# Three edits in TensorE's order of work: a product with its operands exchanged, a moved piece of a projection, two engines' copies exchanged

## What is computed

```
h = RMSNorm(x); proj = h @ w_in           # one projection for all groups
  retention:  rq, rk, rv, rg (4 heads)    # chunk 0: q, k; chunk 1: v, gate
  attention:  fq, fk, fv (8 heads)        # chunks 2, 3, 4
              fl = h @ w_in[:, 8 columns]
              logf = log_sigmoid(fl + fox_f_bias)
  conv:       cb, cc, ch
x = x + concat(retention, attention, conv) @ w_out
x = x + (silu(dwconv3(h2 @ w_gate)) * (h2 @ w_up)) @ w_down,  h2 = RMSNorm(x)
```

## Time and profile before

| | us |
|---|---|
| median of 3 runs | 1617.2 |
| lowest and highest | 1616.39, 1618.21 |
| the profiled execution's own time | 1618.32 |
| its span, first to last instruction | 1616.5 |
| PE busy | 1595.0 (99%), x10304 |
| PEld busy | 1389.9 (86%), x10304 |
| DVE busy | 1080.2 (67%) |
| ACT busy | 687.2 (43%) |
| mean granted TensorE clock | 0.999 |

### The profile page before, as it was taken

How to read it: one execution, slowest core, us unless ns; L and a number is a source line. 1 busy time by engine, 2 the same in 40 slices (tenths; PEclk the granted TensorE clock), 3 DMA queues, 4 the chain that set the end, 5 groups by cost and what they waited for, 6 DMA issues and landing times.

```text
span 1616.5 us, 29200 instructions
## 1 busy us (share of the span) xinstructions
PE 1595.0 (99%) x10304; PEld 1389.9 (86%) x10304; DVE 1080.2 (67%) x1749; ACT 687.2 (43%) x1285; POOL 410.8 (25%) x524
## 2 busy tenths in 40 slices
PE   7999999999999999999999999999999999999998
PEld 6878896688999999999888789867899999999997
DVE  4445447528977777777644553674399777777775
ACT  4224337416544444444433233463264444444442
POOL 1114200004433333333112140010044333333330
PEclk9999999999999999999999999999999999999999
DMA  8223423822222222222242224156213222222222
GB/s 247 79 50 87 137 85 105 301 78 66 79 78 78 85 83 81 90 89 78 72 110 66 70 80 144 66 178 227 85 60 105 85 87 88 78 78 78 78 78 71
DMA packets 125319, 160.04 MB, mean 99 GB/s; under 512 B 25636, under 2 KB 77294, under 8 KB 125166
## 3 DMA queue, kind: packets, MB, share of 16 engines
q1 hardware_dynamic: 125096, 158.65, 32.2%
q10 hardware_dynamic: 144, 0.33, 0.1%
HBM read 149.43 MB, written 9.53 MB: 98 GB/s over the span
## 4 chain that ended last, share of the span: by engine, by line
PE 94%; DVE 2%; ACT 1%; DVEq 1%; issue 1%; DMA 1%; POOL 0%; POOLq 0%; SPq 0%; ACTq 0%
PE bank L2156 89%; PE bank L2218 5%; DVEq L1837 1%; DVE pf L1840 1%; DMA raw<-in_w_in 0%; DVE xn L1505 0%; ACT pf L1284 0%; DMA raw<-in_w_gate 0%; DVE small L1827 0%; DVE hlo L1484 0%; DVE gulo L1484 0%; ACT xn L1152 0%; POOL small L923 0%; ACT hhi L1130 0%; POOLq L1046 0%
## 5 line engine op out<-in xcount | busy, mean ns | idle before, releaser
L2156 PE MATMUL bank<-whi,hhi 128*128 128x512 f32 x560 | 226.7, 405 | 2.4 <-ACT rso L1171 1.1
L2156 PE MATMUL bank<-whi,hlo 128*128 128x512 f32 x560 | 220.2, 393 | 0.0
L2156 PE MATMUL bank<-wlo,hhi 128*128 128x512 f32 x560 | 219.8, 393 | 0.0
L2156 PE MATMUL bank<-hhi,whi 128*128 128x320 f32 x640 | 199.2, 311 | 0.8 <-DVE hlo L1484 0.8
L2156 PE MATMUL bank<-hlo,whi 128*128 128x320 f32 x640 | 198.1, 310 | 0.0
L2156 PE MATMUL bank<-hhi,wlo 128*128 128x320 f32 x640 | 198.0, 309 | 0.0
L2156 PE MATMUL bank<-whi,guhi 128*128 128x512 f32 x440 | 174.1, 396 | 0.4 <-DVE gulo L1484 0.4
L2156 PE MATMUL bank<-wlo,guhi 128*128 128x512 f32 x440 | 173.8, 395 | 0.0
L2156 PE MATMUL bank<-whi,gulo 128*128 128x512 f32 x440 | 173.7, 395 | 0.0
L1460 DVE TENSOR_TENSOR wlo<-raw,whi 128x1024 fp32r<-128x1024 f32 x80 | 100.1, 1252 | 106.1 <-ACT whi L1079 104.8
L1943 DVE TENSOR_TENSOR x<-x,bank 128x512 f32<-128x512 f32 x220 | 143.1, 682 | 39.6 <-PE bank L2156 39.3
(11 more groups left out here) (312 smaller groups left out, 3662.1 us busy)
## 6 DMA issues: line engine op xcount, KB each, us to landing
raw<-in_w_in SPq DMA_DIRECT2D x52, 512.0 KB, 3.7
raw<-in_w_gate SPq DMA_DIRECT2D x44, 512.0 KB, 3.8
raw<-in_w_down SPq DMA_DIRECT2D x44, 512.0 KB, 3.7
vb<-in_cache_fox_v SPq DMA_DIRECT2D x16, 1024.0 KB, 6.8
raw<-in_w_up SPq DMA_DIRECT2D x24, 512.0 KB, 3.8
gains<-in_w_up SPq DMA_DIRECT2D x20, 512.0 KB, 3.8
raw<-in_w_out SPq DMA_DIRECT2D x16, 512.0 KB, 4.8
kb<-in_cache_fox_k SPq DMA_DIRECT2D x8, 1024.0 KB, 6.7
```

What stands on the lines that cost most here:

```text
L2156: return pe.matmul(out, lhsT=lhsT, rhs=rhs, start=start, stop=stop, skip_group_check=True)
```

## The change

Three edits.

**The product.** `fl` becomes one job in one bank. For each of the five token tiles, the tokens' 128 columns of `hhi` and `hlo` are stationary and the 16 columns of `wfl` stream: 80 matmuls with 16 columns in place of 32 with 320. The result is token-major at once; `flT`, its bank's job and the table `fsum` go. ScalarE copies the bank into `flr`, now 128 rows by 5 x 16, and VectorE adds the two parts and then the bias, from SBUF, with a drain between.

**The piece.** The piece of chunk 2 behind `retained(1)` goes, and one comes behind `fill(ins, "rso")`, ahead of `chunk2(0, [3])`. The iterator hands them out in the same order.

**The copies.** From step 2 of the cache sweep on, ScalarE copies the key groups 1 and 3 and VectorE 0 and 2; before, ScalarE 0 and 2 and VectorE 1 and 3.

```diff
@@ plan_banks @@
-    j(("fl", 0), 0)
-    j(("fl", 1), 2)
+    j("fl", 0)
     chunk(1)
     turns("rt")
-    j("flT", 7)
@@ the buffer of the copied product @@
-            [("flr", [2 * FH, NTOK], F32)],
+            [("flr", [P, TT, 2 * FH], F32)],
@@ ScalarE @@
-                for half in range(2):
-                    evac(("fl", half), flr[:, half * HALF:(half + 1) * HALF], l, view=lambda b: b[0:2 * FH, 0:HALF])
+                evac("fl", flr[:, :, :], l, view=lambda b: b[:, 0:TT * 2 * FH].rearrange("p (t n) -> p t n", t=TT))
...
-                        for p_ in (0, 2) if n > 1 else (2, 3) if n == 1 else ():
+                        for p_ in (1, 3) if n > 1 else (2, 3) if n == 1 else ():
@@ VectorE @@
-                B.wait_full(dve, "flT", l)
+                B.wait_taken(dve, "fl", l)
                 dve.wait_ge(foxg_in, l * 64 + 64)
-                dve.tensor_tensor(lf[:, :, :], bank[B.bank("flT")][:, 0:40].rearrange("p (t h) -> p t h", t=TT),
-                                  fbias[:, :].unsqueeze(1).to_broadcast([P, TT, FH]), ALU.add).then_inc(B.free[B.bank("flT")], 1)
+                dve.tensor_tensor(lf[:, :, :], flr[:, :, 0:FH], flr[:, :, FH:], ALU.add)
+                dve.drain()
+                dve.tensor_tensor(lf[:, :, :], lf[:, :, :], fbias[:, :].unsqueeze(1).to_broadcast([P, TT, FH]), ALU.add)
...
-                        for p_ in (1, 3) if n > 1 else (0, 1) if n == 1 else ():
+                        for p_ in (0, 2) if n > 1 else (0, 1) if n == 1 else ():
                             key_copy(n, p_)
@@ TensorE @@
-                for half in range(2):
-                    key = ("fl", half)
-                    B.wait_room(pe, key, l)
-                    ts = slice(half * HALF, half * HALF + HALF)
+                B.wait_room(pe, "fl", l)
+                for t in range(TT):
+                    ts = slice(t * P, (t + 1) * P)
                     for k in range(KT):
                         for h_ in (hhi, hlo):
-                            ins = mm(bank[B.bank(key)][0:2 * FH, 0:HALF], wfl[:, k, :, :].rearrange("p s n -> p (s n)"),
-                                     h_[:, k, ts], k == 0 and h_ is hhi, k == KT - 1 and h_ is hlo)
-                        if half == 1 and k == 3:
+                            ins = mm(bank[B.bank("fl")][:, t * 2 * FH:(t + 1) * 2 * FH], h_[:, k, ts],
+                                     wfl[:, k, :, :].rearrange("p s n -> p (s n)"), k == 0 and h_ is hhi, k == KT - 1 and h_ is hlo)
+                        if t == TT - 1 and k == 3:
                             ins.then_inc(slab_used, 1)
-                    fill(ins, key)
+                fill(ins, "fl")
                 chunk(1, l, "rt", lambda t: pe.wait_ge(rot_ready, l * TT + t + 1))
-                for half in range(2):
-                    B.wait_taken(pe, ("fl", half), l)
...
-                B.wait_room(pe, "flT", l)
-                for t in range(TT):
-                    ins = mm(bank[B.bank("flT")][:, t * FH:(t + 1) * FH], flr[:, t * P:(t + 1) * P], K("fsum")[0:2 * FH, :], True, True)
-                fill(ins, "flT")
...
                 retained(1)
-                piece(l)
...
                 fill(ins, "rso")
+                piece(l)
                 chunk2(0, [3], l)
```

More of the change, by code:

```diff
@@ L78 @@
 for _name, _n in (("ident", P), ("tri", 896), ("cs", TT * 64), ("kdec", TT * RH), ("qdec", 2 * P), ("g16", 2),
-                  ("tris", P), ("bmask", 16), ("e0", P), ("bsel", NB), ("fsum", FH)):
+                  ("tris", P), ("bmask", 16), ("e0", P), ("bsel", NB)):
     CONST[_name] = (_at, _n)
@@ L111, in tables @@
     put("bsel", ((p % HD) // FH)[:, None] == b8[None, :])
-    put("fsum", (p[:, None] < 2 * FH) & (p[:, None] % FH == np.arange(FH)[None, :]))
     dp = np.where(p[None, None, :] >= p[:, None, None],
@@ L603, in build @@
         mark(0, 4, ("c", 0, TT - 1))
-        mark(FL, 2, ("fl", 1))
+        mark(FL, 2, "fl")
         for c in range(1, 5):
```

## The result

The changed kernel takes 1635.22 us (median of 5 runs, 1633.79 to 1636.46) where the kernel before took 1617.20 (5 runs, 1616.39 to 1618.21). The ratio is 1.011, 95% interval 1.0099 to 1.0121: slower by 18 us, 3.3 us less than the forecast of 1638.5 and inside its range. The profiled execution took 1633.79 us, its span is 1632.0 us against 1616.5 before, and TensorE's mean granted clock is 0.990 against 0.999.

A forecast was written before the change was run, and what follows sets the result against it. TensorE's own queue, 94% of the chain of waits, was taken as the bound. 1618.3 + 6.1 (product) + 17.2 (clock) - 1.1 (piece) - 0.8 (fall at 112.21) - 0.9 (keys) = 1638.8, stated as 1638.5 us, range 1626 to 1646.

The forecast's parts named there:

- The static cost of the product: Forget gate's product: 80 load-bound matmuls at 0.112 us replace 5.92 us per layer, +6.1 us in all, bounds +5.0 to +8.2.
- The clock: New product stage and chunk 1 behind it: clock falls part way in both layers, +17.2 us, bounds +11.2 to +22.4.
- the fall after 2.6 us: In the product stage: clock falls after 23 products, taken between 1.8 and 3.4 us; 57 left cost +6.4 us per layer.
- The 2.2 for chunk 1: Chunk 1's dense matmuls begin at the lower clock for 4.4 us, a loss of 2.2 us per layer.
- That the clock holds: Rival for the product stage: gapless weight loads count as work, so the clock stays up; 1621.6 us, chance 9%.
- The piece: Chunk 2 before tile 3: the moved piece removes 0.57 us idle in both layers, -1.1 us, bounds 0 and -1.2.
- The fall at 112.21: Layer 0's dense work behind the 64 small matmuls: half of a 1.6 us clock fall saved, -0.8 us (0 to -1.6).
- The keys: Cache sweep, fourth key group: swapped copies save 0.08 us a step over 12 steps, -0.9 us, bounds -3.1 to +1.2.
- the bound of 3.1: Cache sweep's key copies: best case, the whole 0.26 us stall a step goes, -3.1 us.
- The range's upper end: Whole kernel: up to 1646 us, from 1618.3 + 6.1 + 22.4 with nothing gained elsewhere.
- The rival of a lost cover: Edits don't do what they say, above all chunk 1 or slabs arrive late: some us above forecast or longer falls; 3%.

The follow-up runs named there:

- wide streams: The changed kernel with each of the 80 products streaming 256 columns of `hhi` in place of 16 of `wfl`: 1621.34 us, ratio 1.0031.
- interleaved kernel: The changed kernel with its 80 products five at a time between chunk 0's dense triples: 1629.89 us; later variants with 25 or 10 products behind chunk 0: 1631.06, 1625.92.

## Why the prediction was right

**The static cost of the product** was forecast at 0.112 us each and +6.1 us in all. Measured: 0.112 to 0.113 each while the clock was up (34 in layer 0, 20 in layer 1), so 80 x 0.112 - 4.71 - 1.21 = 3.04 per layer. The 1.21 us of `flT` are confirmed by the wide streams' run, where chunk 1 to `rT` takes 32.42 (56.60 to 89.02) in place of 33.67, 1.25 less. The best row was that of the step removed by the change. The Trainium skill's figure of 81 ns a matmul (TensorE: Matmul & The Clock Gate, "Back-to-back issue gap") is not what this stage shows: 0.112 us, with fp32r operands.

**The clock** was forecast to fall in both layers, part way, at 8.6 us each (+17.2). It fell in both, in both profiles with the stage as the change has it. The size is 14.7: in layer 0, 46 products at 0.213 in place of 0.112 make 4.7, and the dense matmuls behind them 1.8 (0.62 + 1.21 for the `flT` that is gone); in layer 1, 60 products make 6.1 and the dense ones 2.1. The terms that were mis-sized: the fall after 2.6 us was 3.8 in layer 0 and 2.3 in layer 1 (46 and 60 products left where 57 were forecast), and a low product costs 0.101 more, not 0.112. The 2.2 for chunk 1 was nearly right. The 2.6 was a choice between two ways of counting one earlier fall, and the runs show that the moment isn't fixed, so that the size came near is in part luck.

**That the clock holds**, because the loads leave no gap, was the first rival. The stage had no gap (PEld busy 3.82 of 3.82 and 9.82 of 9.82), and the clock fell in it. The Trainium skill's account of falls by idle gaps (the same page, "HAM oscillation — how this bites in real kernels") doesn't cover this case: its trace disagrees. The time that the rival gave, 1621.6, is near where the wide streams came out (1621.34): that kernel is the change with the clock held, though its products cost 0.009 us more each, 1.4 us in all.

**The piece** was forecast at -1.1. From the 64 small matmuls' start to the dense one it is 1.97 us in place of 2.62 (118.16 - 116.19), 0.65 per layer, so -1.3: somewhat over the idle alone. **The fall at 112.21** was given half of its 1.6; it is gone in every profile with the piece moved, though also in that of the product alone, where the piece stands in its old place. In the profiled pair all of it was gained: counted from the first `rT`, the matmul at 111.98 before is reached 0.70 us earlier after the change (120.11), the one at 115.58 2.24 earlier (122.17), so the term was 1.5 where 0.8 was forecast. As the kernel before has the fall in only part of its executions, the medians gain less by it.

**The keys** were forecast at -0.9; the trace of the keys alone gives 0.8, and the groups of single times 0.5 to 0.9. The reading that VectorE's copy, though it starts earlier, also takes longer was right; the bound of 3.1 was out of reach for this edit, though not for the order of TensorE's work.

**A term that the forecast doesn't have** is a wait for `pf` in layer 0, 0.4 us (1.2 in 5 waits before, 0.8 in 4 after). The wait (at 257.56 in the kernel before) stands in all five profiles with the old product and in none of the seven with the exchanged one. So it went with that edit; by what path was not traced.

**The sum** by these readings: 6.1 + 14.7 - 1.3 - 1.5 - 0.8 - 0.4 = 16.8, less 0.7 that the first wait was shorter in this execution makes 16.1, where the spans differ by 15.5. The 0.6 left over is within what unedited work varies by: the feed-forward, from the last transposes of `xn` to `last`, takes 411.94 and 412.25 us in the two layers before and 412.18 and 411.15 after, and between 411.15 and 412.52 in all twelve profiles. The forecast for the profiled execution, 1638.8, was 5.0 us above its 1633.8: 2.5 is the clock's term, 0.7 the fall at 112.21, 0.4 the wait for `pf`, 0.7 the first wait, and the rest is the leftover and the rounding of the small terms. The large parts err to the same side.

**The range's upper end** was added up too low: 1618.3 + 6.1 + 22.4 is 1646.8, and with the upper bound of the static term, 8.2, it would be 1648.9. The result lies far from it.

**The rival of a lost cover** (chunk 1 or its slabs late) did not come true in the change: with the longer stage there was more time for the split of slab 6, not less. It came true in the interleaved kernels, where the expectation had not asked what the product covered.

## What to carry over

A matmul with a full fp32 stationary tile and a short stream costs its weight load (0.112 us here with 8 or with 16 columns streamed): swapping the operands here cut the streamed columns to an eighth and raised the time from 4.7 us to 9 at full clock. Keep the wide operand streaming, the more so as a long stage of short streams dropped the clock here, for itself and for the dense work behind it, which was most of the loss. Before a stage is moved, list which copies on other engines finish under it; and where a ring of banks stalls, look for work in TensorE's own queue that can go in between before changing which engine copies.

## What was not expected of the hardware

- The clock fell in a stage with no gap, after 3.8 and 2.3 us of it, and stayed down 13.65 and 17.07 us, including about 4 us of dense matmuls. With 256 columns behind the same loads it stayed at 1.00.
- The profile's clock column doesn't show every slow stretch. At the kernel's start dense matmuls start 0.43 us apart (12.68, 13.11, 13.54 and on to 16.10), as at the lower clock, while the window 14.00:16.00 shows PEclk 1.00. The prediction went by the starts there; a mean clock of 1.000 says nothing of that stretch.
- At the lower clock a load-bound product takes 0.213 us against 0.112: the load slows with the clock as the stream does.
- A start flag clears more than its own columns. In the interleaved kernel five sums of 16 columns each were open at once in one bank, each with a start flag of its own. The log-forget values of the four prompt tiles, begun earlier, came out off by 0.53 of their size, and those of the fifth tile, begun last, by 3e-6: the earlier sums had lost their first half. With one flag at the very first product all five keep both halves, at the same time of 1629.89 us. The Trainium skill says so of the whole bank (PSUM — Partial Sum Buffer, "The four PSUM rules"), and this pair of kernels agrees.
